# Hybrid decoder block with expert retrieval: 64 tokens instead of 32 get their down products by gathers, and 32 of the last block's dots are done in the top-16 stage

## The chip, the cores and the metric

The kernel runs on 1 core of a Trainium2 chip (trn2). The metric is device time in microseconds (us) of one execution; the profile shows one such execution.

The engines are PE (TensorE, matmuls; its weight loads are listed as PEld), DVE (VectorE), ACT (ScalarE), POOL (GpSimd) and SP (SyncE, which only issues transfers). Sixteen DMA engines move data for the queues of SP, ACT and POOL.

## The reference, cut to what matters

512 tokens of width 1024 go through an attention layer and then through a retrieval layer, which is the part that the change touches:

```
def peer_ffn(h, w_query, sub_keys_1, sub_keys_2, expert_down, expert_up):
    q = (ht @ w_query).reshape(N, PEER_HEADS, 2, PEER_QDIM // 2)      # N 512, 8 heads
    s1 = einsum('nhd,kd->nhk', q[:, :, 0], sub_keys_1)                # 128 keys
    s2 = einsum('nhd,kd->nhk', q[:, :, 1], sub_keys_2)
    t1, i1 = top_k(s1, 16);  t2, i2 = top_k(s2, 16)
    cand = t1[..., :, None] + t2[..., None, :];  sc, pos = top_k(cand, 16)
    eidx = (i1 * 128 + i2) at pos                                     # 128 * 128 = 16384 experts
    gate = softmax(sc)
    ...
        u = expert_down[e_c]                                          # rows of 1024
        a = gelu(einsum('cd,chkd->chk', x_c, u))
        vv = expert_up[e_c]
        return einsum('chk,chkd->cd', g_c * a, vv)
```

Each token picks 16 experts in each of 8 heads, 128 in all. For each it needs a dot product of its own vector with the expert's down row, a gelu, a gate, and the sum of the weighted up rows.

## The kernel before

Tokens lie in four blocks of 128. The last block (tokens 384 to 511) is handled by **gathers**: POOL fetches the picked down row of each of the 128 tokens (one indirect transfer of 128 rows, 512 KB), DVE takes the dot with the token's own vector (`dot`, or `pick` with kind "D"), and later POOL fetches the up rows and DVE adds them up (`pick` with kind "U"). The first three blocks (TD = 384 tokens) are handled **densely**: PE multiplies all 16384 experts with these tokens, 128 experts at a time (`score_block`), and the gate stage builds from one-hot matrices which of the products count.

The last XT = 32 tokens of the third block are a mixed case: their down products are not taken from the dense products but by gathers and dots as well, so `score_block` has TN = 384 - 32 = 352 token columns. XG = 128 / XT of their picks share a transfer, one per group of XT partitions, so these tokens cost XP = 128 / XG = 32 gathers ("X" picks). What they need is their gelu'd dots, moved back to their own partitions (`x_act`), multiplied into the gates (`x_w`) and put in place by one-hot matmuls of three bf16 parts instead of two f16 parts (`one_hots_extra`).

The stages around the change, in order of time:

- **The top-16 stage** (300 to 500 us). PE runs 16 rounds of query products, key scores and one `score_block` (numbers 2 to 17), then further blocks alone. DVE finds the top 16 of each head, eight heads one after the other, and the row numbers. `slots_T` on PE, in the middle of block E_SLOTS, transposes the result of the last head; only then can DVE make one-hot matrices.
- **The gate stage** (518 to 778 us): 12 groups of 32 tokens. Per group DVE makes four one-hot or weighted matrices of 128 x 4096 f16 (`one_hots`), PE multiplies them (64 matmuls) and runs some score blocks, `early_to(i)` says how far; ACT copies the gates out and stores them. Between the matrices DVE does the blocks' low parts (`d_low`) and the early dots.
- **The up stage** (778 to 1487 us): PE adds the up products of two numbers e per pair (`add_up`, 18 matmuls of 512 columns each), DVE makes their weights (`w_e`, `w_lo_e`) and low parts (`u_lo`), and the rest of the last block's picks; `units_by(e)` sets how many picks are done by number e. From number NE on, the pair also holds two score blocks and their `d_low`.

Every block e is three products: high part of the weights with high and low part of the tokens (L2050, 16 matmuls), low part of the weights with the high part of the tokens (L2062, 8). The high part is a rounding copy on ACT (`d_high`), and the low part is what is left. There are three ways to make it: DVE subtracts (`d_low`, blocks from E_DVE on), POOL subtracts (`early_low`), or, for ACC_FROM <= f < ACC_TO, ACT writes the negated rounded weights into `d_sum` and a POOL-issued transfer adds `d_raw` to it on its way (an **accumulate**, L660):

```
                if summed(f):
                    pool.wait_ge(S("d_hi_done"), f + 1)
                    pool.dma_start(d_sum[f % 3][:], d_raw[f % DR][:], accum_op=ALU.add)\
                        .then_inc(S(f"f_summed{f % 3}"), 16)
                    return
```

All queues are written out by hand and run in that order; nothing is scheduled. `d_raw` has 4 buffers (DR), `d_hi` and `d_sum` 3, gathered rows 4 in the gate stage (`e_in`) and 8 in the up stage (`p_in`). Block f's weights are loaded once block f - 4 is done; its high part is made once block f - 3 is done.

## Time and profile before

| | before |
|---|---|
| median of 3 runs | 1490.92 us (1490.85 to 1492.23) |
| the profiled execution | 1488.97 us, span 1487.2 us, granted clock 0.998 |
| PE / DVE / ACT / POOL busy | 98% / 82% / 42% / 37% of the span |
| moved by DMA | 412.08 MB, mean 277 GB/s |
| score blocks before the gates / up to the up stage / in it | 29 / 53 / 46 |
| gathers in the gate stage / in the up stage | 48 / 240 |

The span is from the first to the last instruction; the execution's own time is 1.8 us longer. A busy PE is not a PE at its peak, since its matmuls are pipelined: the distance between the starts of two matmuls is what one costs, not its duration. DMA share is the mean over the 16 engines of the time in which packets were under way; it can exceed 1 a little, since packets overlap.

### The profile page before, as it was taken

What the parts mean: (1) busy time and instruction counts of PE and PEld (TensorE: products, weight loads), DVE (VectorE), ACT (ScalarE), POOL (GpSimd) and SP (SyncE); (2) the same over time, 40 slices, a digit from 0 to 9 for tenths busy, and PEclk for the clock granted to TensorE, in tenths of its full rate; (3) what the DMA queues carried; (4) which work ended last, traced back from release to release, by engine and by line L of the source; (5) the groups of instructions that cost most, each with busy time, mean ns of one, the idle gap of its engine ahead of it and who ended that gap; (6) DMA issues with size and microseconds to landing.
All of it is one profiled execution on the core that took longest, in us unless ns stands there. A gap on an engine that the chain in (4) does not pass through costs nothing.

```text
span 1487.2 us, 22558 instructions
## 1 busy us (share of the span) xinstructions
PE 1459.3 (98%) x8412; PEld 1301.0 (87%) x8412; DVE 1220.5 (82%) x2396; ACT 629.3 (42%) x1003; POOL 551.8 (37%) x369
## 2 busy tenths in 40 slices
PE   9999999999999999999899999999999999999998
PEld 6887888798989999999897888888888998998996
DVE  5577886439999989998937888888879999999996
ACT  6237675343332445454543333333334334334334
POOL 0324101132312444543004444454426565667530
PEclk9999999999999999999999999999999999999999
DMA  7403003275555699999779999999999999999971
GB/s 308 163 1 114 1 1 131 70 191 167 166 142 145 220 346 389 377 373 356 295 274 394 387 378 370 382 360 384 377 412 331 400 373 409 368 403 380 392 283 71
DMA packets 140541, 412.08 MB, mean 277 GB/s; under 512 B 13553, under 2 KB 62321, under 8 KB 137489
## 3 DMA queue, kind: packets, MB, share of 16 engines
q1 hardware_dynamic: 81920, 206.08, 37.3%
q0 software_dynamic: 44256, 164.25, 30.3%
q10 hardware_dynamic: 14256, 40.31, 7.4%
q8 instruction: 67, 1.10, 0.3%
q14 instruction: 42, 0.34, 0.1%
HBM read 358.57 MB, written 42.04 MB: 269 GB/s over the span
## 4 chain that ended last, share of the span: by engine, by line
PE 81%; DVE 9%; DMA 6%; ACT 2%; issue 1%; SPq 0%; ACTq 0%; DVEq 0%
PE bank L2152 22%; PE bank L2050 16%; PE bank L1771 12%; PE bank L2158 11%; PE bank L2062 8%; DMA d_raw<-down 3%; PE bank L2122 3%; PE bank L1982 2%; PE bank L1966 1%; DMA w_raw<-wts 1%; PE bank L1891 1%; DVE gp L1645 1%; DMA a_e<-act_dram 1%; PE bank L2071 1%; DVE e_in L1586 1%
## 5 line engine op out<-in xcount | busy, mean ns | idle before, releaser
L2050 PE MATMUL bank<-h_hi,d_hi 128*128 128x352 f32 x1024 | 330.6, 324 | 2.8 <-ACT f_act L950 1.8
L2050 PE MATMUL bank<-h_lo,d_hi 128*128 128x352 f32 x1024 | 327.9, 321 | 0.0
L702 POOL DMA_INDIRECT p_in<-up,p_row x128 | 181.4, 1417 | 155.2 <-DVE xt L1677 76.5
L702 POOL DMA_INDIRECT p_in<-rows,p_row x112 | 163.9, 1463 | 180.4 <-DVE p_dot L1671 67.3
L2050 PEld LDWEIGHTS bank<-h_hi,d_hi 128*128 128x128 f32 x1024 | 191.7, 187 | 4.3 <-issue 3.3
L2050 PEld LDWEIGHTS bank<-h_lo,d_hi 128*128 128x128 f32 x1024 | 191.7, 187 | 1.1
L2152 PE MATMUL bank<-u_hi,w_hi_e 128*128 128x512 f32 x750 | 191.1, 390 | 1.0 <-DVE w_lo_e L1704 1.0
L2152 PE MATMUL bank<-u_hi,w_lo_e 128*128 128x512 f32 x750 | 190.6, 389 | 0.0
L2158 PE MATMUL bank<-u_lo,w_hi_e 128*128 128x512 f32 x750 | 190.5, 389 | 0.0
L1677 DVE SCALAR_TENSOR_TENSOR xt<-p_in,p_w,xt 128x1024 f32<-128x1024 f32 x128 | 164.2, 1283 | 6.8
L918 ACT ACTIVATE d_hi<-d_raw 128x1024 fp32r<-128x1024 f32 x128 | 132.4, 1053 | 87.6 <-DMA d_raw<-down 66.9
L2152 PEld LDWEIGHTS bank<-u_hi,w_lo_e 128*128 128x128 f32 x750 | 140.8, 188 | 29.8
L2158 PEld LDWEIGHTS bank<-u_lo,w_hi_e 128*128 128x128 f32 x750 | 140.8, 188 | 29.2
L2152 PEld LDWEIGHTS bank<-u_hi,w_hi_e 128*128 128x128 f32 x750 | 140.1, 188 | 29.1 <-ACT u_hi L998 1.3
L1570 DVE TENSOR_TENSOR u_lo<-u_raw,u_hi 128x1024 fp32r<-128x1024 f32 x128 | 152.4, 1221 | 13.4 <-ACT u_hi L998 13.4
L2062 PE MATMUL bank<-h_hi,d_lo 128*128 128x352 f32 x888 | 160.1, 321 | 0.0
L1575 DVE TENSOR_TENSOR d_lo<-d_raw,d_hi 128x1024 fp32r<-128x1024 f32 x102 | 122.5, 1221 | 35.1 <-ACT d_hi L918 35.1
L1040 ACT ACTIVATE w_hi_e<-w_e 128x768 fp32r<-128x768 f32 x64 | 54.3, 848 | 221.7 <-DVE w_e L1697 220.9
L2062 PEld LDWEIGHTS bank<-h_hi,d_lo 128*128 128x128 f32 x888 | 145.0, 187 | 0.0
L998 ACT ACTIVATE u_hi<-u_raw 128x1024 fp32r<-128x1024 f32 x128 | 130.2, 1048 | 19.2 <-PE bank L2158 18.1
L1671 DVE CUSTOM_DVE_ANT_0 p_in<-p_in,h_row 128x1024 f32<-128x1024 f32 x112 | 132.9, 1222 | 0.0
L1697 DVE TENSOR_TENSOR w_e<-a_e,g_e 128x768 f32<-128x768 f32 x64 | 61.3, 957 | 68.5 <-DMA a_e<-act_dram 38.7
(328 smaller groups left out, 2412.0 us busy)
## 6 DMA issues: line engine op xcount, KB each, us to landing
d_raw<-down SPq DMA_DIRECT2D x128, 512.0 KB, 6.9
u_raw<-up SPq DMA_DIRECT2D x128, 512.0 KB, 6.8
gates_dram<-ev ACTq DMA_DIRECT2D x12, 2048.0 KB, 7.0
g_e<-gates_dram SPq DMA_DIRECT2D x60, 384.0 KB, 9.1
w_raw<-wts SPq DMA_DIRECT2D x9, 2048.0 KB, 9.0
act_dram<-f_act ACTq DMA_DIRECT2D x82, 176.0 KB, 5.9
a_e<-act_dram SPq DMA_DIRECT2D x41, 352.0 KB, 8.1
d_sum<-d_raw POOLq DMA_DIRECT2D x17, 512.0 KB, 5.3
```

Source lines behind the costliest of these rows:

```text
L702: pool.indirect_dma_start(out=p_in[n % GR][:], out_offset=None, in_=rows if kind == "D" else up.rearrange("n p d -> (n p) d"), in_offset=b ...
L918: nc.scalar.activation(d_hi[e % DH_R][:], d_raw[e % DR][:], ACT.Copy).then_inc(S("d_hi_done"), 1)
L998: nc.scalar.activation(u_hi[e % UH][:], u_raw[e % UR][:], ACT.Copy).then_inc(S("u_hi_done"), 1)
L1570: V.tensor_tensor(u_lo[e % UR][:], u_raw[e % UR][:], f32(u_hi[e % UH][:]), ALU.subtract)\
L1575: V.tensor_tensor(d_lo[e % DR][:], d_raw[e % DR][:], f32(d_hi[e % DH_R][:]), ALU.subtract)\
L1671: V.tensor_tensor_reduce(out=rows_in[:], in0=rows_in[:], in1=h_row[:], scale=1.0, scalar=0.0, op0=ALU.mult, op1=ALU.add, accum_out=p_dot[: ...
L1677: V.scalar_tensor_tensor(xt[:, TDB], rows_in[:], p_w[:, p:p + 1], xt[:, TDB], ALU.mult, ALU.add)\
L1771: m = nc.tensor.matmul(out, a, b, start=(n == 0 and j == 0), stop=(n == last and j == 2))
L2050: nc.tensor.matmul(bank[6 + e % 2][:, 0:TN], d_hi[e % DH_R][:, k], h[:, k, 0:TN], start=(k == j == 0), stop=False)
L2062: m = nc.tensor.matmul(bank[6 + e % 2][:, 0:TN], low[:, k], h_hi[:, k, 0:TN], start=False, stop=(k == KC - 1))
L2152: nc.tensor.matmul(bank[2 * b + half][:], w[e // 2 % 2][:, e % 2, b * P:(b + 1) * P], u_hi[e % UH][:, half * COLS:(half + 1) * COLS], star ...
L2158: m = nc.tensor.matmul(bank[2 * b + half][:], w_hi_e[e // 2 % 2][:, e % 2, b * P:(b + 1) * P], u_lo[e % UR][:, half * COLS:(half + 1) * CO ...
```

## The change

XT becomes 64: TN falls to 320 columns, the X picks become XP = 64 gathers in two groups of partitions, and two of the twelve gate groups (instead of one) are made of three parts. The down dots of the last block's first two heads (EARLY_D = 32 instead of 16, out of the last block's 128) move out of the gate stage into the top-16 stage: DVE works out their rows after heads 0 and 1 (`t_row`), POOL gathers them into three new buffers (`t_in`) between its other work, and DVE takes the dots between the steps of heads 2 to 7. `slots_T` moves from block 24 to block 39, the accumulates cover blocks 3 to 35 instead of 3 to 19, and the first eight gate groups hold six blocks instead of five, so that NE goes from 82 to 104 and 24 instead of 46 blocks are left for the up stage. The up stage's picks fall from 240 to 224 and their plan changes.

```
-XT = 32
+XT = 64
 XG = P // XT
 XP = PICKS // XG
 TN = TD - XT
 XGRP = NTG - XT // TG
-EARLY_D = 16
-E_PICKS = [("D", p) for p in range(4)] + [("X", n) for n in range(XP)] + [("D", p) for p in range(4, EARLY_D)]
+EARLY_D = 32
+E_PICKS = [("D", p) for p in range(EARLY_D)] + [("X", n) for n in range(XP)]
+def e_slot(m):
+    return m % 3 if m < EARLY_D else (m - EARLY_D) % 4
+def gather_at(m):
+    return 8 + m * 3 // 5 if m < 21 else 20 + (m - 21) * 8 // 5
+def dots_at(n):
+    return range(EARLY_D * n // 18, EARLY_D * (n + 1) // 18) if n >= 0 else ()
...
-X_GELU = X_GROUPS
+X_GELU = X_GROUPS - 1
...
-E_SLOTS = 24
+E_SLOTS = 39
 E_DVE = E_SLOTS + 2
 E_GATES = E_SLOTS + 5
-ACC_FROM, ACC_TO = DH_R, 20
+ACC_FROM, ACC_TO = DH_R, E_SLOTS - 3
...
-    return E_GATES + 5 * min(i, X_GROUPS) + 2 * max(0, i - X_GROUPS)
+    return E_GATES + 6 * min(i, X_GROUPS) + 2 * max(0, i - X_GROUPS)
...
-        return max(0, e - 3) * 6 // 5
+        return max(0, e - 3) * 10 // 7
     last = NK - 4
-    start = (NE - 4) * 6 // 5
+    start = (NE - 4) * 10 // 7
     return min(len(ORDER), start + -(-(e - NE + 1) * (len(ORDER) - start) // (last - NE)))
...
             for f in range(E_DVE):
                 early_low(f)
+                for m in range(EARLY_D):
+                    if gather_at(m) == f:
+                        if m % TOPK == 0:
+                            pool.wait_ge(S("t_rows"), m // TOPK + 1)
+                        if m >= 3:
+                            pool.wait_ge(S("x_used"), m - 2)
+                        gather(m)
...
             pool.wait_ge(S("rows_ready"), 1)
-            for m, (kind, p) in enumerate(E_PICKS):
+            pool.wait_ge(S("x_used"), EARLY_D)
+            pool.wait_ge(S("pd_done"), ACC_TO)
+            pool.wait_ge(S("x_moved"), 16 * (2 * XG - 1))
+            for m in range(EARLY_D, len(E_PICKS)):
...
                 for f in range(early_to(i), early_to(i + 1)):
                     early_step(f)
+                    if f == early_to(X_GELU) + 4:
+                        extra_gelu()
...
+                    for m in dots_at(3 * hd - 6 + s):
+                        dot(m)
...
+                for m in dots_at(3 * hd - 4):
+                    dot(m)
...
+                if hd < EARLY_D // TOPK:
+                    dve.wait_ge(S("key_done"), 2 * hd + 2)
+                    V.scalar_tensor_tensor(t_row[:, hd * TOPK:(hd + 1) * TOPK], key[0][:, TDB, hd], float(NK), key[1][:, TDB, hd],
+                                           ALU.mult, ALU.add).then_inc(S("t_rows"), 1)
...
                 def between(n):
                     for _ in range(n):
+                        for _ in range(2 if i == X_GROUPS else 1):
+                            if dots:
+                                dot(dots.pop(0))
                         if lows:
                             d_low(lows.pop(0))
-                        if dots:
-                            dot(dots.pop(0))
```

Left out of this diff are the places of small tiles in SBUF and the semaphore counts that go with `e_slot`.

What POOL's queue holds around the end of the 16 rounds, before: `d_sum` are accumulates, `d_lo` are subtractions on POOL itself, and `e_in` the first early gathers, which stand behind all of them.

```order
L660 DMA d_sum_204<-d_raw_197 128x1024
L660 DMA d_sum_202<-d_raw_199 128x1024
L660 DMA d_sum_203<-d_raw_201 128x1024
L664 TENSOR_TENSOR d_lo_194<-d_raw_195,d_hi_207 128x1024
L664 TENSOR_TENSOR d_lo_196<-d_raw_197,d_hi_205 128x1024
L664 TENSOR_TENSOR d_lo_198<-d_raw_199,d_hi_206 128x1024
```

The same queue in the changed kernel, from block 24 on: `t_in` are the gathers of the last block's first two heads.

```order
L690 DMA d_sum_206<-d_raw_199 128x1024
L714 DMA t_in_148<-rows,t_row 128x1024
L690 DMA d_sum_207<-d_raw_201 128x1024
L690 DMA d_sum_208<-d_raw_203 128x1024
L714 DMA t_in_176<-rows,t_row 128x1024
L690 DMA d_sum_206<-d_raw_205 128x1024
L690 DMA d_sum_207<-d_raw_199 128x1024
L714 DMA t_in_177<-rows,t_row 128x1024
L690 DMA d_sum_208<-d_raw_201 128x1024
L714 DMA t_in_148<-rows,t_row 128x1024
```

From block 20 to block 35 every low part is now an accumulate with gathers between them, and POOL subtracts itself only from block 36 on.

DVE's queue for one gate group, before, from the second matrix on: `oh` and `gp` are the matrices, `e_dot` rows are the dots (each with a row that reads the accumulator).

```order
L1640 TENSOR_TENSOR oh_215<-iota_k,sl_key_175 128x4096
L1575 TENSOR_TENSOR d_lo_200<-d_raw_201,d_hi_207 128x1024
L1586 ISA e_in_233,e_dot<-e_in_233,x_home 128x1024
L1575 TENSOR_TENSOR d_lo_194<-d_raw_195,d_hi_205 128x1024
L1586 ISA e_in_230,e_dot<-e_in_230,x_home 128x1024
...
L1643 TENSOR_TENSOR gp_218<-oh_214,sl_g_176 128x4096
L1575 TENSOR_TENSOR d_lo_196<-d_raw_197,d_hi_206 128x1024
...
L1645 TENSOR_TENSOR gp_219<-oh_214,sl_g_177 128x4096
```

And in the changed kernel, from the third matrix of a group on:

```order
L1703 TENSOR_TENSOR gp_224<-oh_220,sl_g_180 128x4096
L1537 ISA e_in_237,e_dot<-e_in_237,x_home 128x1024
L1646 TENSOR_TENSOR d_lo_204<-d_raw_205,d_hi_211 128x1024
L1537 ISA e_in_234,e_dot<-e_in_234,x_home 128x1024
L1646 TENSOR_TENSOR d_lo_198<-d_raw_199,d_hi_209 128x1024
L1537 ISA e_in_235,e_dot<-e_in_235,x_home 128x1024
L1646 TENSOR_TENSOR d_lo_200<-d_raw_201,d_hi_210 128x1024
L1537 ISA e_in_236,e_dot<-e_in_236,x_home 128x1024
...
L1537 ISA e_in_237,e_dot<-e_in_237,x_home 128x1024
...
L1705 TENSOR_TENSOR gp_225<-oh_220,sl_g_181 128x4096
```

A group holds eight dots and six low parts instead of six and five, the dot now stands ahead of the low part, and the last five dots of a group stand close together, over a ring of four `e_in` buffers.

## Rows read from the trace of the kernel before

**Rows 1.** The page, busy time of PE, its weight loads and DVE.

```profile
PE 1459.3 (98%) x8412; PEld 1301.0 (87%) x8412; DVE 1220.5 (82%) x2396; ACT 629.3 (42%) x1003; POOL 551.8 (37%) x369
```

**Rows 2.** Busy time by stretch; the last columns are granted clock, DMA share, GB/s.

```profile
466.00:500.00 34.00, 31.62 (x202) 31.28 (x200) 33.62 (x151) 14.46 (x18) 14.78 (x6) 1.00 0.60 176
...
518.00:704.00 186.00, 184.35 (x1473) 182.36 (x1470) 168.78 (x168) 91.23 (x145) 85.10 (x44) 1.00 0.96 367
...
778.00:1102.00 324.00, 323.05 (x1427) 267.29 (x1427) 267.42 (x298) 110.33 (x122) 137.45 (x98) 1.00 1.01 382
1102.00:1436.00 334.00, 334.00 (x1767) 303.48 (x1766) 309.38 (x341) 120.02 (x154) 206.90 (x143) 1.00 0.99 381
```

**Rows 3.** Chain that ended last: start us, us, what; blocks and gate groups.

```profile
618.85 2.56 PE bank L2050 x16
621.41 1.28 PE bank L2062 x8
...
680.70 3.69 PE bank L2122 x64
...
744.63 7.21 PE bank L2122 x96
```

**Rows 4.** The same chain in the up stage.

```profile
861.63 2.72 PE bank L2152 x12
...
865.71 2.72 PE bank L2152 x12
```

**Rows 5.** Timeline of DVE at the end of the top-16 stage.

```profile
489.35 3.48 DVE L1454 TENSOR_TENSOR hit<-place_h,ranks 128x1024 f16<-128x1024 f16 x2
...
499.45 0.69 DVE L1553 TENSOR_TENSOR score<-score,g_sum 128x512 f32<-128x512 f32 x1
```

**Rows 6.** DMA queues from 357 to 364 us: packets, MB, share; issues, median landing.

```profile
q0 software_dynamic: 144, 0.52, 37.8%
q1 hardware_dynamic: 144, 0.52, 30.1%
q10 hardware_dynamic: 144, 0.18, 7.0%
...
d_sum<-d_raw POOLq DMA_DIRECT2D x1, 512.0 KB, 6.1
```

**Rows 7.** DMA queue of the gathers, 1102 to 1436 us; and the fastest 24.5 us.

```profile
q0 software_dynamic: 20437, 74.42, 58.1%
...
1236.00:1260.50 24.50, 24.50 (x133) 22.42 (x133) 23.13 (x21) 8.40 (x13) 15.06 (x14) 1.00 1.03 415
```

**Rows 8.** Timeline of DVE in a gate group; landing of the early gathers.

```profile
564.22 2.29 DVE L1638 TENSOR_TENSOR oh<-iota_k,sl_key 128x4096 f16<-128x4096 f16 x1
566.42 1.22 DVE L1575 TENSOR_TENSOR d_lo<-d_raw,d_hi 128x1024 fp32r<-128x1024 f32 x1
567.55 1.22 DVE L1586 CUSTOM_DVE_ANT_1 e_in<-e_in,x_home 128x1024 f32<-128x1024 f32 x1
568.70 2.29 DVE L1640 TENSOR_TENSOR oh<-iota_k,sl_key 128x4096 f16<-128x4096 f16 x1
...
e_in<-rows,e_row POOLq DMA_INDIRECT x32, 9.9
```

**Rows 9.** Timeline in the up stage, one pair: DVE, and PE's next block.

```profile
1162.35 0.96 DVE L1697 TENSOR_TENSOR w_e<-a_e,g_e 128x768 f32<-128x768 f32 x1 [0.98 <-ACT a_e L1035]
1163.23 1.28 DVE L1677 SCALAR_TENSOR_TENSOR xt<-p_in,p_w,xt 128x1024 f32<-128x1024 f32 x1
1164.42 0.99 DVE L1704 TENSOR_TENSOR w_lo_e<-w_e,w_hi_e 128x768 fp32r<-128x768 f32 x1
1165.34 2.35 DVE L1575 TENSOR_TENSOR d_lo<-d_raw,d_hi 128x1024 fp32r<-128x1024 f32 x2
...
1169.87 0.32 PE L2050 MATMUL bank<-h_hi,d_hi 128*128 128x352 f32 x1
1169.88 8.22 DVE L1677 SCALAR_TENSOR_TENSOR xt<-p_in,p_w,xt 128x1024 f32<-128x1024 f32 x6
```

More of the change, by code:

```diff
@@ L676, in w_low, with gather @@
                 ins.then_inc(S("w_part_lo"), 1)
+            def gather(m):
+                kind, p = E_PICKS[m]
+                slot = e_slot(m)
+                early = m < EARLY_D
+                rows_at = t_row if early else e_row
+                pool.indirect_dma_start(
+                    out=(t_in if early else e_in)[slot][:], out_offset=None, in_=rows,
+                    in_offset=bass.IndirectOffsetOnAxis(ap=rows_at[:, p:p + 1], axis=0)).then_inc(S(f"p_loaded{slot}"), 16)
             for f in range(E_DVE):
                 early_low(f)
+                for m in range(EARLY_D):
[5 more added lines that the diff above has]
+                        gather(m)
                 n, part = divmod(f - E_AHEAD, 4)
@@ L998, in u_high, with extra_gelu @@
                 nc.scalar.activation(u_hi[e % UH][:], u_raw[e % UR][:], ACT.Copy).then_inc(S("u_hi_done"), 1)
+            def extra_gelu():
+                last = slice(P - XT, P)
+                act.wait_ge(S("x_used"), len(E_PICKS))
+                nc.scalar.activation(e_act[0:P - XT], e_dot[0:P - XT], ACT.Gelu).then_inc(S("x_gelu"), 1)
+                nc.scalar.activation(x_act[last, PICKS - XP:], e_dot[last], ACT.Gelu).then_inc(S("x_gelu"), 1)
+                act.wait_ge(S("x_gelu"), 1)
+                for g in range(XG - 1):
+                    act.dma_start(x_act[last, g * XP:(g + 1) * XP], e_act[g * XT:(g + 1) * XT])\
+                       .then_inc(S("x_moved"), 16)
             for i in range(NTG):
@@ L1476, in keys_of, with dot @@
                      .then_inc(S("key_done"), 1)
+            def dot(m):
+                kind, p = E_PICKS[m]
+                slot = e_slot(m)
+                by_k = lambda t: t[:].rearrange("p (k d) -> p k d", k=KC)
+                to, own = (e_dot, x_home) if kind == "X" else (p_dot, by_k(h_row))
+                rows_in = by_k((t_in if m < EARLY_D else e_in)[slot])
+                dve.wait_ge(S(f"p_loaded{slot}"), e_loads(m, slot))
+                if (kind, p) == ("X", 0):
+                    dve.wait_ge(S("x_homed"), 16)
+                V.tensor_tensor_reduce(out=rows_in, in0=rows_in, in1=own, scale=1.0, scalar=0.0,
+                                       op0=ALU.mult, op1=ALU.add, accum_out=to[:, p:p + 1])\
+                 .then_inc(S("x_used"), 1)
             def top16(vals, idx, src, tmp):
```

62 lines of the change are left out of this document (24 added, 38 removed).

## The prediction

> **What bounds the kernel now.** I read the page first: PE is busy for 98% of the span [rows 1]. The reader is to see in that row that the weight loads leave room and that DVE, at 82%, is the next engine. The busy time by stretch then shows where each engine stands [rows 2]: PE works without a gap from 1102 to 1436 us, loses 1 us from 778 to 1102 and 2.4 us from 466 to 500, where it waits for the top-16 stage. In the same rows the DMA share is 0.96 in the gate stage and about 1 in the up stage, at 367 to 382 GB/s, and DVE is busy for 309 of 334 us in the second half of the up stage. So PE sets the end, and two resources stand right behind it. The chain that ended last gives PE's true prices, since it lists what one piece adds: a score block is 2.56 + 1.28 = 3.84 us for 24 matmuls of 352 columns, 160.2 ns each [rows 3]. In the up stage 12 matmuls of 512 columns add 2.72 us, 226.7 ns each, and one expert number takes 4.08 us (865.71 - 861.63) [rows 4]. The difference is 66.5 ns for 160 columns, 0.416 ns a column.
>
> **What PE gains.** 32 columns fewer take 13.3 ns from each matmul of a block: 24 x 128 = 3072 matmuls, **-41.0 us**. A block then costs 3.52 us. A gate group of three parts takes PE 7.21 us where one of two parts takes 3.69 [rows 3]; there is one more: **+3.5 us**. The 2.4 us wait at the old place of `slots_T` [rows 2] should go, because 15 more blocks of 3.52 us (53 us) stand before it, while DVE gets 32 dots of 1.15 us (37 us): **-2.4 us**. That DVE no longer meets POOL's subtractions (the pair of f16 products took 3.48 us at 489 us, beside them) [rows 5] only makes DVE earlier, and I give it nothing. DVE ended this work at about 500 us [rows 5]; with 37 us more it ends at about 537. PE had come to the middle of block 24 about 2.4 us before DVE's end, near 497.5; 24.5 blocks that are 0.32 us shorter and 15 more of 3.52 bring it to the middle of block 39 at 497.5 - 7.8 + 52.8 = 542, if nothing stops it.
>
> **What stops it: the accumulates, +25 us.** Blocks 20 to 35 now run back to back and each needs an accumulate, where before all but two of those after the rounds were subtracted on POOL. The DMA queues of one round show their price [rows 6]: in 7 us the accumulate's queue (q0) held the engines for 37.8%, 2.65 us, for 0.52 MB; the weight load (q1) for 2.1 us; the store of the products (q10) for 0.49 us. Nothing else ran, and the accumulate landed 6.1 us after its issue. A saturated queue of gathers costs 58.1% of 334 us for 143 gathers, 1.36 us each, and the fastest long stretch moved 415 GB/s at a share of 1.03 [rows 7]. A block of this stretch thus asks for 2.65 us (accumulate), 0.524 MB / 415 GB/s = 1.26 us (its load, taken at the saturated rate since the queues are full then), 0.44 us (store of 320 columns) and 11 gathers / 16 blocks x 1.36 = 0.94 us: 5.29 us, or 5.1 us at a share of 1.03, against PE's 3.52. Sixteen blocks lose 16 x 1.6 = 25 us. The rings of 3 and 4 buffers let it run two or three blocks ahead, so little can be saved up. PE stands in L2062 meanwhile, and behind it wait `slots_T`, then DVE with the whole gate stage; DVE's own last dots wait too, for gathers that stand behind the accumulates in POOL's queue. Bounds: 0, if accumulates overlap with other packets, and 16 x (6.2 - 3.52) = 43 us with the load at its 2.1 us and the store at 0.49.
>
> A rule speaks for a much lower price. The Trainium skill (DMA: Bandwidth & Descriptors, Bandwidth) says that transfers from SBUF to SBUF are bound by the fabric at 435 GB/s; by that an accumulate holds the engines for an estimated 1.2 us, not 2.65, and this term would be 4 us. The row contradicts it here: 0.52 MB in 2.65 us is about 200 GB/s.
>
> **The gate stage, +16 us.** A matrix costs DVE 2.20 us from start to start (564.22 to 566.42), a low part 1.13 and a dot 1.15 [rows 8]. Before: 4 x 2.20 + 5 x 1.13 + 6 x 1.15 = 21.4 us a group, against PE's 3.69 + 5 x 3.84 = 22.9. After: 8.8 + 6 x 1.13 + 8 x 1.15 = 24.8 us against 3.69 + 6 x 3.52 = 24.8. DVE's slack is gone. Yet it cannot run without stops: it idled 17.2 us in the eight groups of before [rows 2], 2.1 us each, for high parts whose weights come through a ring of four. These stops had lain in the slack; now each pushes the next matrices. I take 2 us x 8. Bounds: 0, if a later DVE finds its high parts ready, and 27 us from the ring of four gather buffers: the last dot of a group follows the one four before it by 3 x 2.28 + 1.15 = 8.0 us in DVE's order, but a freed buffer is full only 9.9 us after the next issue [rows 8], 11.4 us with the dot and the hand-over: 3.4 us x 8. The new waits behind the dots (`extra_gelu` on ACT) stand where all dots are done; nothing for them.
>
> **The up stage, +2 and +12 us.** First part: 10/7 instead of 6/5 picks a number, 2.86 a pair. DVE needs 0.88 + 0.92 + 2 x 1.13 + 2.86 x 1.17 = 7.4 us of 8.16 [rows 8, 9]; the transfers (two up loads, gates, products, gathers) are 3.27 MB in 8.16 us, 400 GB/s, between the 382 of this stretch now and the best 415 [rows 2, 7]: +2, bounds 0 and 11 (at 390 GB/s). Second part: 82 picks in ten pairs, 32 dots and 50 up rows. Up rows in a row cost 8.22 / 6 = 1.37 us each [rows 9]. DVE: 32 x 1.15 + 50 x 1.37 + 10 x (1.80 + 4 x 1.13) = 168.5 us; PE: 10 x (8.16 + 7.04) = 152. DVE may fall about 5 us behind before PE notices, since it starts a pair's low parts at 1165.34 and PE's next block starts at 1169.87 and needs the low part 2.6 us later, less the product's time [rows 9]: +12, bounds 5 and 17.
>
> **Sum**, against the profiled execution (1488.97 us; its span is 1487.2): -41.0 + 3.5 - 2.4 + 25 + 16 + 2 + 12 = +15, 1504 us. The median shown lies 1.95 us above that execution: **1506 us**, slower by 1.0%.
>
> **The rivals.** (a) An accumulate costs the engines no more than a copy, 1.26 us: a block asks 3.8 us, the term is 4 and the time 1485. For it: the measured round was partly idle. Against it: its queue alone held them 2.65 us. This is the case by the Trainium skill's fabric rule named above. It decides from a block of 3.95 us: below that the change is faster by over 0.2%. (b) The top-16 stage slips, but gate and up stage keep PE's pace but for 5 us: -41.0 + 3.5 - 2.4 + 25 + 5, 1481 us. For it: DVE stops for high parts because it comes early. (c) Nothing slips but a few us at the end: the columns' gain stays, 1454 us. For it: shares near 1 have not stopped PE so far. (d) The upper bounds come together in the top-16 and gate stages: 43 + 27 instead of 25 + 16, 1535 us.
>
> **How the numbers follow.** Forecast 0.46 (its own range 1492 to 1522), (a) 0.13, (b) 0.12, (c) 0.15, (d) 0.14. A measurement of this kernel tells about 0.2% from no change. Faster: all of (b) and (c), most of (a): 0.34; same: 0.08, from the edges of (a) and the forecast; slower 0.58. The range reaches from the upper part of (c) to the lower part of (d): 1458 to 1528.
>
> **What would show it.** Right: blocks 20 to 35 start about 5 us apart with PE waiting for the transfer into `d_sum`; DMA share about 1 there; the transposes of `slots_T` near 567 us; gate groups 26 to 28 us apart; PE gaps for `d_lo` or `w_lo_e` in the last ten pairs before the end. Wrong: blocks 3.5 us apart in that stretch and transposes near 542 us would take away the largest loss; gate groups at 24.8 us apart the second. If `score_block`'s matmuls do not come 147 ns apart, the gain itself was mis-sized.

## The result

The changed kernel takes **1546.93 us** (median of 4 runs, 1542.98 to 1548.80) against 1490.88 us: ratio **1.0372**, 95% interval 1.0357 to 1.0387. It is slower by 3.7%, where 1.0% was forecast, and it lies beyond the range (1458 to 1528 us). The profiled execution took 1547.79 us, with a span of 1545.9 us.

The page of the changed kernel (busy time, then the DMA total), beside [rows 1]:

```profile
PE 1441.7 (93%) x8444; PEld 1275.7 (83%) x8444; DVE 1245.9 (81%) x2448; ACT 642.0 (42%) x1019; POOL 616.5 (40%) x416
DMA packets 153454, 441.80 MB, mean 286 GB/s; under 512 B 14688, under 2 KB 69088, under 8 KB 150400
```

PE's busy share falls from 98 to 93%: the columns were saved and more than given back in waits. The view of one source line shows where. Each row has the first and the last start of a matmul: the transposes of `slots_T`, the gate matmuls, and the up stage's first product.

```profile
L2164 PE MATMUL bank<-cst,score x3: 421/421/476, 589.0 to 589.4; 128*128 128x128 f32 x3
L2182 PE MATMUL bank<-gp,oh x640: 218/218/308, 606.7 to 852.8; 128*128 128x128 f16 x160
L2212 PE MATMUL bank<-u_hi,w_hi_e x750: 387/389/472, 904.9 to 1523.6; 128*128 128x512 f32 x188
```

The same rows of the kernel before:

```profile
L2104 PE MATMUL bank<-cst,score x3: 272/273/329, 500.2 to 500.5; 128*128 128x128 f32 x3
L2122 PE MATMUL bank<-gp,oh x704: 217/218/233, 517.9 to 734.0; 128*128 128x128 f16 x176
L2152 PE MATMUL bank<-u_hi,w_hi_e x750: 387/389/467, 778.6 to 1464.8; 128*128 128x512 f32 x188
```

That cuts the span into three stages. "Without losses" is the length before, with the blocks between the two marks counted anew (3.84 us each out, 3.52 in: 53 and 60 in the gate stage, 46 and 24 in the up stage) and 3.5 us for the third part; for `slots_T` it is the prediction's 542.

| stage | before | without losses | after | lost | forecast |
|---|---|---|---|---|---|
| `slots_T` at | 500.2 | 542 | 589.0 | 47 | 25 |
| first gate matmul to up stage | 260.7 | 271.9 | 298.2 | 26 | 16 |
| up stage, first to last | 686.2 | 594.0 | 618.7 | 25 | 14 |

All three lost more than forecast, and the first misses most, 22 us. So most runs went there.

What engines waited for from 465 to 605 us in the changed kernel (total us, times, longest):

```profile
POOL d_sum L690 <- ACT d_hi L963: 63.9, 16, 12.7
DVE t_in L1537 <- DMA t_in<-rows,t_row: 42.2, 8, 9.6
PE bank L2122 <- DMA d_sum<-d_raw: 24.7, 10, 5.5
PE bank L2164 <- DVE score L1624: 5.5, 1, 5.5
```

In the changed kernel's numbering L2122 is a block's product with its low part (L2062 before), L2110 the one with its high part (L2050 before), and L2164 the transposes. Both PE and DVE stand still there: PE for accumulates, DVE for its gathers. ACT's timeline gives the blocks one by one, since each has one high part. Blocks 19, 20, 22, 23, 35 and 39:

```profile
456.25 1.04 ACT L963 ACTIVATE d_hi<-d_raw 128x1024 fp32r<-128x1024 f32 x1
...
472.67 1.04 ACT L963 ACTIVATE d_hi<-d_raw 128x1024 fp32r<-128x1024 f32 x1
...
482.62 1.04 ACT L963 ACTIVATE d_hi<-d_raw 128x1024 fp32r<-128x1024 f32 x1
496.27 1.05 ACT L963 ACTIVATE d_hi<-d_raw 128x1024 fp32r<-128x1024 f32 x1
...
557.45 1.04 ACT L963 ACTIVATE d_hi<-d_raw 128x1024 fp32r<-128x1024 f32 x1
...
574.99 1.06 ACT L963 ACTIVATE d_hi<-d_raw 128x1024 fp32r<-128x1024 f32 x1 [0.46 <-DMA d_raw<-down]
```

From 23 to 35 a block takes 61.18 / 12 = **5.10 us**, the forecast's number. But block 20 is late, there is a hole of 13.65 us before block 23, and `slots_T` comes 14 us behind block 39's high part.

Why block 20 is late can be read from PE's timeline, here the key scores of two rounds (eight matmuls, the same work both times):

```profile
463.60 2.08 PE L2131 MATMUL bank<-sk,q_sb 128*128 128x128 f32 x8 [3.67 <-DVE ti L1556]
...
470.60 1.05 PE L2131 MATMUL bank<-sk,q_sb 128*128 128x128 f32 x8
```

PE waits 3.7 us for DVE, which is late in the rounds, and then works slowly for a while: the key scores take 1.0 us more than the next ones, and the 16 matmuls on the high part behind them 1.6 us more than those of the next block (3.92 and 2.35 us). The granted clock from 464 to 468 us was 0.50, and 1.00 from 472 to 476 us. Wait and slow clock together are 6.3 us, and block 20 comes 6.4 us later behind block 19 than the rounds' usual 10.0 us.

### The profile page after: what moved, and what is told of

Read it like the earlier page. It is cut to its first block, busy times and chain, and to the rows that moved or that the text cites. A ratio compares the mean times of both kernels' runs of the same rounds, so it can differ in the third digit from the quotient of the medians.

```text
span 1545.9 us, 22788 instructions
## 1 busy us (share of the span) xinstructions
PE 1441.7 (93%) x8444; PEld 1275.7 (83%) x8444; DVE 1245.9 (81%) x2448; ACT 642.0 (42%) x1019; POOL 616.5 (40%) x416
## 4 chain that ended last, share of the span: by engine, by line
PE 46%; DVE 26%; DMA 19%; issue 3%; POOL 2%; ACT 2%; SPq 1%; DVEq 0%; ACTq 0%
PE bank L2212 14%; PE bank L1831 8%; PE bank L2218 7%; DMA a_e<-act_dram 5%; PE bank L2110 5%; DMA e_in<-rows,e_row 5%; DVE xt L1737 4%; DMA d_raw<-down 3%; PE bank L2122 3%; DVE d_lo L1646 3%; DVE e_in L1537 3%; PE bank L2042 2%; POOL p_in L747 2%; DMA t_in<-rows,t_row 2%; DMA d_sum<-d_raw 2%
## 5 line engine op out<-in xcount | busy, mean ns | idle before, releaser
L2110 PE MATMUL bank<-h_hi,d_hi 128*128 128x320 f32 x1024 | 310.8, 316 | 17.3 <-ACT d_hi L963 14.9
L2110 PE MATMUL bank<-h_lo,d_hi 128*128 128x320 f32 x1024 | 306.2, 312 | 0.0
L747 POOL DMA_INDIRECT p_in<-up,p_row x128 | 189.9, 1484 | 149.5 <-DVE xt L1737 68.6
L2110 PEld LDWEIGHTS bank<-h_hi,d_hi 128*128 128x128 f32 x1024 | 196.2, 192 | 22.7 <-ACT d_hi L963 20.5
L747 POOL DMA_INDIRECT p_in<-rows,p_row x96 | 157.6, 1642 | 117.0 <-DVE p_dot L1731 49.6
L2110 PEld LDWEIGHTS bank<-h_lo,d_hi 128*128 128x128 f32 x1024 | 196.4, 192 | 0.1
L2212 PEld LDWEIGHTS bank<-u_hi,w_hi_e 128*128 128x128 f32 x750 | 139.5, 188 | 38.5 <-ACT u_hi L1043 10.4
L2218 PEld LDWEIGHTS bank<-u_lo,w_hi_e 128*128 128x128 f32 x750 | 140.8, 188 | 29.2
L714 POOL DMA_INDIRECT e_in<-rows,e_row x64 | 103.4, 1616 | 131.8 <-DVE e_dot L1537 122.2
L2122 PE MATMUL bank<-h_hi,d_lo 128*128 128x320 f32 x760 | 128.8, 312 | 6.1 <-DVE d_lo L1646 6.1
L1646 DVE TENSOR_TENSOR d_lo<-d_raw,d_hi 128x1024 fp32r<-128x1024 f32 x87 | 104.7, 1220 | 24.9 <-ACT d_hi L963 24.8
L2122 PEld LDWEIGHTS bank<-h_hi,d_lo 128*128 128x128 f32 x760 | 116.7, 190 | 6.9 <-DVE d_lo L1646 6.9
L1731 DVE CUSTOM_DVE_ANT_0 p_in<-p_in,h_row 128x1024 f32<-128x1024 f32 x96 | 114.4, 1217 | 4.5 <-DMA p_in<-rows,p_row 4.5
```

What stands on the lines that cost most here:

```text
L747: pool.indirect_dma_start(out=p_in[n % GR][:], out_offset=None, in_=rows if kind == "D" else up.rearrange("n p d -> (n p) d"), in_offset=b ...
L1646: V.tensor_tensor(d_lo[e % DR][:], d_raw[e % DR][:], f32(d_hi[e % DH_R][:]), ALU.subtract)\
L1731: V.tensor_tensor_reduce(out=rows_in[:], in0=rows_in[:], in1=h_row[:], scale=1.0, scalar=0.0, op0=ALU.mult, op1=ALU.add, accum_out=p_dot[: ...
L2110: nc.tensor.matmul(bank[6 + e % 2][:, 0:TN], d_hi[e % DH_R][:, k], h[:, k, 0:TN], start=(k == j == 0), stop=False)
L2122: m = nc.tensor.matmul(bank[6 + e % 2][:, 0:TN], low[:, k], h_hi[:, k, 0:TN], start=False, stop=(k == KC - 1))
L2212: nc.tensor.matmul(bank[2 * b + half][:], w[e // 2 % 2][:, e % 2, b * P:(b + 1) * P], u_hi[e % UH][:, half * COLS:(half + 1) * COLS], star ...
```

## The experiments

All times are medians; "ratio" is that to the kernel before, which was run again beside them (medians 1488.79 to 1491.18 us). The stage lengths come from the same three rows as above. Runs are of the changed kernel with the edit named. The stage lengths are those of one profiled execution, whose time lies up to 6.7 us from the median of its run (e1_pool_sub 1531.99 us, e2_even 1535.70, e20_paced_25 1492.39), so a difference of a few us between two stage lengths says little by itself. Three runs leave work out to price it: e4_copy the addition, e7_no_gathers 29 of the 32 early gathers, e18_nog_copy both.

| run | us | ratio, interval | `slots_T` at | gate stage | up stage |
|---|---|---|---|---|---|
| changed kernel | 1546.93 | 1.0372 (1.0357 to 1.0387) | 589.0 | 298.2 | 618.7 |
| e1_pool_sub | 1538.64 | 1.0333 (1.0315 to 1.035) | 575.9 | 298.9 | 614.6 |
| e4_copy | 1528.90 | 1.0283 (1.0254 to 1.0313) | 568.9 | 295.0 | 619.0 |
| e2_even | 1530.78 | 1.0273 (1.0256 to 1.029) | 587.1 | 283.9 | 621.5 |
| e3_iota | 1548.07 | 1.0385 (1.0364 to 1.0407) | 589.0 | 297.6 | 620.1 |
| e7_no_gathers | 1517.96 | 1.0203 (1.0167 to 1.0239) | 559.8 | 296.6 | 617.4 |
| e5_alt_even | 1525.47 | 1.0247 (1.0215 to 1.0278) | 574.0 | 286.6 | 619.3 |
| e6_slope32 | 1540.00 | 1.0319 (1.0278 to 1.036) | 590.5 | 296.3 | 610.7 |
| e9_slope43 | 1553.28 | 1.0417 (1.0391 to 1.0443) | 586.3 | 296.5 | 628.3 |
| e10_deep_ring | 1541.72 | 1.0343 (1.0319 to 1.0368) | 582.0 | 301.2 | 619.4 |
| e11_deep_even_slope | 1515.00 | 1.0178 (1.0159 to 1.0196) | 580.0 | 283.5 | 610.7 |
| e12_deep_even_slope_alt | 1507.84 | 1.0126 (1.0103 to 1.0149) | 575.6 | 283.9 | 609.7 |
| e13_xt32 | 1534.96 | 1.0295 (1.027 to 1.0319) | 589.9 | 278.0 | 626.1 |
| e18_nog_copy | 1507.00 | 1.0108 (1.0079 to 1.0136) | 551.5 | 298.5 | 619.6 |
| e15_half_early | 1511.02 | 1.015 (1.0113 to 1.0188) | 549.3 | 289.7 | 633.0 |
| e16_half_early_28 | 1502.76 | 1.0091 (1.0065 to 1.0116) | 528.3 | 292.5 | 638.5 |
| e17_half_early_alt | 1506.13 | 1.0118 (1.0081 to 1.0155) | 540.9 | 289.8 | 636.1 |
| e19_paced | 1498.39 | 1.0046 (1.0029 to 1.0062) | 524.9 | 288.4 | 647.8 |
| e20_paced_25 | 1498.02 | 1.0063 (1.0037 to 1.0089) | 513.2 | 285.1 | 651.8 |

### What an accumulate costs

**e1_pool_sub**: POOL subtracts blocks 20 to 35 again.

```
-ACC_FROM, ACC_TO = DH_R, E_SLOTS - 3
+ACC_FROM, ACC_TO = DH_R, 20
```

> The changed kernel with the accumulates given back for blocks 20 to 35: POOL subtracts there, as it did before the change; all else as changed. Theory A (an accumulate holds the DMA engines for 2.65 us or more, so blocks 23 to 35 stand 5.1 us apart): without them a block asks the engines for 2.6 us, the blocks go at PE's 3.5 to 3.7 us, 12 x 1.5 = 18 us are saved there, and the transposes of slots_T come near 568 us instead of 589: 1547 - 20 = 1527 us (1520 to 1535; DVE loses some us beside POOL's subtractions). Theory B (the accumulates are not what holds the stretch, but the loads behind the late constants or DVE's wait for its own gathers): under 6 us saved, 1541 or more.

`slots_T` came 13 us earlier, at 576 instead of the expected 568, and the median fell by 8 us, less than theory A's 12 to 27 and more than theory B's 6: neither theory. The windows of this run (PE, PEld, DVE, ACT, POOL busy; clock; DMA share; GB/s) show that another engine took over:

```profile
520.00:540.00 20.00, 17.64 (x121) 17.38 (x119) 19.96 (x58) 7.50 (x10) 9.83 (x5) 0.99 0.78 255
540.00:560.00 20.00, 14.44 (x85) 14.44 (x86) 19.93 (x79) 4.93 (x7) 18.10 (x9) 0.75 0.56 171
```

DVE is busy without a gap and the DMA engines are at 0.56 to 0.78. DVE waited 1.7 us for its gathers from 465 us on, instead of 42.2, and PE waited 7.0 us for DVE's `score` at `slots_T`; 14.4 us more it waited for POOL's low parts, which stand in POOL's queue behind gathers that wait for DVE's dots (up to 10.4 us). The same work takes DVE longer beside POOL's subtractions; the line that adds up the candidates, for one, here and in the changed kernel:

```profile
L1576 DVE TENSOR_TENSOR cand<-tv,tv 128x64 f32<-128x64 f32 (+1 forms) x40 | 20.6, 579 | 0.1
```
```profile
L1576 DVE TENSOR_TENSOR cand<-tv,tv 128x64 f32<-128x64 f32 (+1 forms) x40 | 8.5, 277 | 0.1
```

In all, DVE was busy 301 us from 200 us to `slots_T`, against 275. So the way out of the accumulates costs DVE 26 us in a stage where it has none to spare.

**e4_copy**: the same transfer without adding.

```
-pool.dma_start(d_sum[f % 3][:], d_raw[f % DR][:], accum_op=ALU.add)\
+pool.dma_start(d_sum[f % 3][:], d_raw[f % DR][:].bitcast(F32R))\
```

> The changed kernel, but each accumulate is a plain copy of the same 0.52 MB between the same two tiles (the low part of a down matrix is then wrong: nothing is added). Theory A as I wrote it in the prediction, with the accumulate as something dearer than a copy (2.65 against 1.26 us of the engines): blocks 23 to 35 come 3.9 us apart instead of 5.1, 12 x 1.2 = 14 us less, 1533 us (1528 to 1538). Theory C (it is the transfer from SBUF to SBUF through this queue that costs about 2.65 us, whether it adds or not): blocks still 5 us apart, 1543 to 1549 us.

20 us earlier at `slots_T`, and 1529 us lies in theory A's range: it is the adding that costs, not the way from SBUF to SBUF. Theory C is out. The gathers stand in the same queue, so the price was taken in a pair of runs without them:

**e7_no_gathers** and **e18_nog_copy** (the latter with the copy besides):

```
-                    if gather_at(m) == f:
+                    if gather_at(m) == f and m < 3:
```

> The changed kernel without 29 of the 32 early gathers: the 32 dots of the top-16 stage are all done, but from the fourth on over what stands in the three buffers, so the last block's first heads get wrong values. It tells which of two chains sets the transposes of slots_T. Theory A (the accumulates starve PE, and DVE's 50.7 us of waits for its gathers only fill time that PE loses anyway): slots_T moves only by what the gathers' bytes take from the DMA engines, about 11 x 1.36 = 15 us in that stretch, most of it hidden: slots_T at 578 to 584 us, 1535 to 1541 us. Theory D (DVE's chain sets it: it waits for gathers that stand in POOL's queue behind accumulates, which wait for high parts, which wait for loads): DVE now ends at about 540 us, PE alone decides, and slots_T comes at 563 to 575 us, when PE has block 39: 1520 to 1533 us.

> The changed kernel without 29 of the 32 early gathers (as in the run without gathers) and with plain copies for accumulates: the low parts and the first heads of the last block are wrong. Against the run without gathers (blocks 23 to 35 4.44 us apart, slots_T at 559.8 us, 1518 us) it gives the accumulate's price by itself. If a copy holds the engines 1.3 to 1.5 us, a block asks for 1.4 + 1.5 + 0.45 = 3.4 us: blocks at PE's 3.5 to 3.7 us, slots_T at 545 to 550 us, 1503 to 1508 us. If a copy costs as much as an accumulate, nothing changes: 1516 to 1520 us.

The queues from 480 to 530 us without gathers (packets, MB, share of 16 engines), q0 being accumulates alone and q1 the blocks' loads:

```profile
q0 software_dynamic: 1601, 5.84, 59.9%
q1 hardware_dynamic: 1671, 6.06, 34.0%
q10 hardware_dynamic: 1675, 1.90, 10.7%
```

and with copies:

```profile
q0 software_dynamic: 1781, 6.44, 36.2%
```

5.84 MB are 11.1 accumulates of 0.524 MB, in 0.599 x 50 = 30 us: **2.69 us each**. A copy: 18.1 us for 12.3, **1.47 us**. A load is 17.0 us for 11.6, also 1.47 us, and not the 1.26 that I took. An accumulate thus moves 195 GB/s and a copy 356. The Trainium skill (DMA: Bandwidth & Descriptors, Bandwidth) gives 435 GB/s for transfers within SBUF; the copy comes to four fifths of that, and the accumulate to under half, so for the accumulate the measured price decides. Rival (a) of the prediction falls with that.

### What the gathers cost

Without gathers `slots_T` comes at 559.8 us, 29.2 us earlier and earlier than either theory had it. Blocks 20, 22, 23, 35 and 39 of e7_no_gathers:

```profile
468.06 1.04 ACT L963 ACTIVATE d_hi<-d_raw 128x1024 fp32r<-128x1024 f32 x1
...
477.28 1.05 ACT L963 ACTIVATE d_hi<-d_raw 128x1024 fp32r<-128x1024 f32 x1
...
483.89 1.05 ACT L963 ACTIVATE d_hi<-d_raw 128x1024 fp32r<-128x1024 f32 x1
...
537.21 1.04 ACT L963 ACTIVATE d_hi<-d_raw 128x1024 fp32r<-128x1024 f32 x1
...
551.36 1.06 ACT L963 ACTIVATE d_hi<-d_raw 128x1024 fp32r<-128x1024 f32 x1 [0.46 <-ACT f_act L995]
```

So the 29 us are: 4.6 up to block 20 (in the changed kernel it stands 16.4 instead of 10.0 us behind block 19; of these 6.4 us 1.8 do not show, since this run's blocks are 1.8 us late from the start, before any gather); 0.7 from 20 to 22; 7.0 between 22 and 23 (6.6 instead of 13.65); 7.9 from 23 to 35 (4.44 us a block instead of 5.10); 3.4 from 35 to 39; and 5.6 behind block 39, where in the changed kernel PE waits 5.5 us for DVE's `score`. Only the third item stood in my sum, there with 0.94 us a block for the 0.66 measured. Two ways by which gathers cost were then separated, bytes and order.

**e10_deep_ring**: from the 22nd gather on a ring of eight buffers, in memory that the last projection has left.

```
-    return m % 3 if m < EARLY_D else (m - EARLY_D) % 4
+    return m % 3 if m < FAR else (m - FAR) % 8 if m < EARLY_D else (m - EARLY_D) % 4
...
-    return 8 + m * 3 // 5 if m < 21 else 20 + (m - 21) * 8 // 5
+    return 8 + m * 3 // 5 if m < FAR else 20 + m - FAR
```

> The changed kernel with eight instead of three buffers for the early gathers from the 22nd on (they lie where the last projection's weights lay, free once the 16 rounds are done), and these eleven gathers issued at blocks 20 to 30 instead of 20 to 36. Bytes, accumulates and dots are the same; only the order and the waits of POOL's queue change. Theory D (the gathers cost so much because POOL's queue ties DVE to PE: accumulates wait behind gathers that wait for dots, and dots wait for gathers that stand behind accumulates): slots_T at 568 to 575 us instead of 589, 1527 to 1534 us. Theory B2 (it is their bytes alone, 0.52 MB each on full DMA engines): slots_T at 583 or later, 1541 or more.

Between the two: 7 us. DVE now was done 26 us ahead and waited for ACT's exponentials, which stand in ACT's queue behind block 38:

```profile
DVE g_sum L1630 <- ACT score L1032: 25.9, 1, 25.9
PE bank L2130 <- DMA d_sum<-d_raw: 23.2, 12, 5.6
```

PE's own wait for accumulates stayed at 23 us. So DVE's chain (the order of POOL's queue) made up about 7 of the 29 us at the end of the stage. The other 22 us are then bytes and what the last rounds lose; no run parts these two.

**e3_iota** was a miss in my reading:

> The changed kernel with the load of iota_k (1 MB) issued at block 39 instead of block 22, that is after the stretch of accumulates instead of at its head. Theory A (the late constants stand ahead of the down loads in SP's queue, which put 13.7 us between the high parts of blocks 22 and 23 where later ones are 5.1 apart; the iota is two thirds of their bytes): block 23 comes 5 to 6 us earlier, the transposes of slots_T near 584 us, 1541 to 1543 us. Rival (the transposes wait for DVE, whose last dots wait for gathers, so that an earlier block 23 changes nothing): 1546 to 1548 us. A rise above 1549 would say that the iota now comes too late for the first gate matrix.

Nothing moved, and the hole before block 23 stayed (483.36 to 496.35 us). The rows of the two transfers in the changed kernel's DMA view from 474 to 497 us (KB, us from issue to landing) show why it could tell nothing:

```profile
x_home<-x_h SPq DMA_DIRECT2D x1, 512.0 KB, 18.0
iota_k<-consts_h SPq DMA_DIRECT2D x1, 64.0 KB, 17.0
```

The iota is 64 KB and not 1 MB; `x_home` is the large one. By itself it makes no hole either: in e18_nog_copy the same load stands there, and blocks 22 and 23 are 5.1 us apart (475.12 to 480.20).

The queues of the same stretch, 474 to 497 us, say more (packets, MB, share):

```profile
q0 software_dynamic: 864, 3.15, 57.9%
q1 hardware_dynamic: 1752, 2.67, 32.9%
q10 hardware_dynamic: 536, 0.60, 7.2%
```

The engines have hardly a gap: the shares add up to 98%. In that time three accumulates, three gathers, four blocks' loads and the two transfers above were issued, since the blocks follow each other faster once the rounds are over. Block 23's own load was issued at 478.73 us, right behind those two, and took 16.55 us. Over all runs the distance of blocks 22 and 23 goes with what is issued there: 9.9 to 14.7 us where accumulates and gathers are, 9.0 us with gathers alone (e1_pool_sub), 6.9 with gathers and copies (e4_copy), and 6.6 to 7.0 with accumulates alone.

**e15_half_early**, **e16_half_early_28**, **e17_half_early_alt**: 16 early dots whose gathers fall into the rounds, 32 or 28 blocks before `slots_T`, with the even spread and the 3/2 below; the third with POOL subtracting even blocks.

```
-EARLY_D = 32
+EARLY_D = 16
...
-E_SLOTS = 39
+E_SLOTS = 32
```

> A form of the change with 16 instead of 32 early dots (their gathers all fall into the 16 rounds, where the DMA engines have room), 32 instead of 39 blocks before slots_T, 16 more picks in the up stage, the even spread and 3/2 picks per expert. If the gathers hurt only behind the rounds: block 20 comes near 468 us as in the run without gathers, DVE ends 19 us earlier than with 32 dots, slots_T at 520 to 530 us for 7 blocks fewer; the work that is left for later is PE's own, so the sum is ideal 1451 plus about 10 in the top-16 stage, 10 in the gate stage, 20 in the up stage: 1490 to 1500 us. If 16 gathers among the rounds hurt as they did here and the up stage cannot carry 16 more picks: 1505 to 1515 us.

> As the run before, with 28 blocks before slots_T: four accumulated blocks fewer in the full stretch. If DVE's end (near 520 us) decides slots_T, PE with 28 blocks stands ready at about 510 us and waits some 10 us: 5 us slower than with 32 blocks. If the accumulates still decide, 3 to 5 us faster.

> As the run with 32 blocks, with the even ones of blocks 20 to 28 subtracted by POOL. A block asks for 3.4 us of the DMA engines instead of 4.7, so PE keeps its pace if DVE does: 3 to 8 us faster than with all accumulated. If DVE beside POOL's subtractions sets slots_T: the same, or up to 4 us slower.

1511, 1503 and 1506 us: each block fewer in the full stretch helps (28 against 32: 8 us, more than expected, and DVE again waited 22 us for the exponentials). But block 20's high part came at 485 to 488 us, not 468 (the expectation of e19_paced says 475, which is block 19). POOL's timeline of e16_half_early_28 says why:

```profile
431.12 1.03 POOL L714 DMA_INDIRECT t_in<-rows,t_row  x1 [1.08 <-DVE p_dot L1537]
447.20 0.98 POOL L714 DMA_INDIRECT t_in<-rows,t_row  x1 [15.05 <-DVE p_dot L1537]
448.15 1.04 POOL L690 DMA_DIRECT2D d_sum<-d_raw  x1
```

The gather at 447 us waited 15 us for the dot that frees its buffer, and behind it stood the accumulate that the next round's block needs.

**e19_paced** moves only this: gather m behind block 8 + m. **e20_paced_25** has 25 blocks before `slots_T` as well.

```
-    return 8 + m * 3 // 5 if m < 21 else 20 + (m - 21) * 8 // 5
+    return 8 + m
```

> As the run with 16 early dots and 28 blocks, but gather m stands behind block 8 + m in POOL's queue instead of 8 + 3m/5, so that the dot that frees its buffer is done when POOL comes to it. If the place in the queue was what cost: the rounds are 10 us apart to the end, the high part of block 20 comes at 466 to 468 us instead of 475, slots_T at 520 instead of 528, 1493 to 1497 us. If the bytes cost: no change, 1501 to 1504 us.

> As e19_paced with 25 blocks before slots_T. DVE stood done about 20 us before slots_T with 28; three accumulated blocks fewer there cost the full stretch 3 x 1.6 us less and come back later at PE's own 3.5 us: 1487 to 1493 us, about the kernel before. If DVE now decides slots_T: not faster than e19_paced.

The rounds are even again in e19_paced and block 20 comes in time:

```profile
459.31 1.04 ACT L963 ACTIVATE d_hi<-d_raw 128x1024 fp32r<-128x1024 f32 x1
...
469.29 1.04 ACT L963 ACTIVATE d_hi<-d_raw 128x1024 fp32r<-128x1024 f32 x1
```

Block 20 came 17 us earlier, but the hole before block 23 opened here too (479.60 to 493.21 us, where e16_half_early_28 had 7.0 us), and `slots_T` moved 3.4 us, the time 4.4. Gathers now stand behind blocks 20 to 23 in POOL's queue, where e16_half_early_28 had its last behind block 17. With 25 blocks DVE sets `slots_T` (PE waits 15.5 us for it), and the time stays at 1498; its twelve runs spread from 1489.85 to 1509.35 us, so it can't be told from e19_paced. These are the best forms found: 0.5 to 0.6% slower than the kernel before.

### The gate stage

**e2_even**: the same dots and low parts, two and two behind each matrix.

```
 V.tensor_tensor(oh[r][0][:], iota, cols(sl_key[0]), ALU.is_equal).then_inc(S("oh_a"), 1)
-between(1)
+between(2)
...
-between(max(len(lows), len(dots)))
+between(2)
 V.tensor_tensor(gp[r][1][:], oh[r][0][:], cols(sl_g[1]), ALU.mult).then_inc(S("oh_done"), 1)
+between(max(len(lows), len(dots)))
```

> The changed kernel with the same matrices, low parts and dots in the gate stage, but spread evenly: two dots and two low parts behind each of the four matrices of a group, where the changed kernel has one, two and then five dots in a row. Theory A (the gate groups stand 28.3 us apart instead of 24.8 because the fifth dot in a row needs a buffer of the ring of four that its gather has not filled): two dots per 6.7 us leave 12 us for a reload against 11.4 needed, the groups come 25 to 26 us apart, 8 x 2.5 to 3.3 = 20 to 26 us less: 1521 to 1527 us. Rival (the groups are slow because DVE's work of 24.8 us plus its waits for d_hi, or the DMA share of 0.9, fill them): 28 us apart as before, 1543 or more; slower by a few us if PE now gets its first matrix of a group later.

The chain of waits of the changed kernel, one group:

```profile
646.49 2.20 DVE gp L1703
648.68 1.14 DVE e_in L1537
...
650.10 10.13 DMA e_in<-rows,e_row
...
660.25 1.23 DVE e_in L1537
...
661.48 2.21 DVE gp L1705
```

The last dot of the group is done 12 us behind the one four before it, since its gather takes 10 us after that buffer is free. This holds in every group, 28.4 us apart (633.04, 661.48, 689.67). With the even spread PE's gate matmuls come:

```profile
606.28 3.69 PE bank L2183 x64
...
632.17 3.90 PE bank L2183 x64
...
658.71 3.69 PE bank L2183 x64
...
684.79 3.68 PE bank L2183 x64
...
692.08 9.43 DMA d_raw<-down
```

26.2 us apart, and the stage is 14.3 us shorter; the time, 1530.8 us, is 4 us above the expected range. The ring of four gather buffers was the cause of that part. What follows in the chain is the load of a block's weights, 9 to 10 us in a ring of four, so that this is the next limit; no run changed that ring. Both periods, 28.4 and 26.2 us, lie above DVE's and PE's 24.8 us.

**e5_alt_even** adds POOL's subtraction for even blocks from 20 on.

```
-    return ACC_FROM <= f < ACC_TO
+    return ACC_FROM <= f < ACC_TO and (f < 20 or f % 2 == 1)
```

> The changed kernel with two edits: of blocks 20 to 35 only the odd ones are accumulated, the even ones subtracted by POOL; and the even spread of the dots in the gate stage. Theory A: a block of this stretch asks the DMA engines for 5.3 - 2.65 / 2 = 4.0 us instead of 5.3; eight POOL subtractions cost DVE half of the 26 us that sixteen cost it (301 us busy up to slots_T against 275). slots_T at 565 to 572 us, 17 to 24 less than 589, and with the 16 us of the even spread 1507 to 1514 us. Rival (DVE beside POOL's subtractions becomes the bound as it did with all sixteen): slots_T at 576, 1518 to 1522 us.

5 us less than the even spread alone, and `slots_T` at 574, about where e1_pool_sub had it: half of the subtractions give as much there as all. `slots_T` lies between the theory's 565 to 572 us and the rival's 576, the time 3 us above the rival's range.

### The up stage

**e6_slope32** and **e9_slope43**: 3/2 or 4/3 instead of 10/7 in `units_by`.

> The changed kernel with 3/2 instead of 10/7 picks per expert in the first part of the up stage: 150 instead of 142 picks there, 74 instead of 82 in the last ten pairs. By the prediction's terms the last ten pairs lose 8 x 1.37 = 11 us of DVE's work there, of which up to 11 come off the time. If the first part (1.03 share of the DMA engines at 390 to 400 GB/s) has no room, it pays 8 x 0.52 MB / 400 GB/s = 10.5 us for them: net 1545 to 1549 us. If it has room, 1536 to 1540 us.

> The changed kernel with 4/3 instead of 10/7 picks per expert in the first part of the up stage: 133 instead of 142 there, 91 instead of 82 in the last ten pairs. If the first part's 9 us of PE's waits come from full DMA engines, 9 gathers fewer give nearly all of them back, while the last ten pairs get 9 x 1.37 = 12 us more: 1547 to 1552 us. If the first part's waits have another cause (the activations' loads come late in SP's queue whatever the bytes), only the 12 us are seen: 1556 to 1560 us.

The up stage is 8.0 us shorter with 8 picks fewer in the last ten pairs, and 9.6 longer with 9 more: 1.0 us for each pick that is moved. e6_slope32 comes out at 1540 us, the edge of what was expected if the first part has room (its four runs spread from 1531.5 to 1542.3 us); e9_slope43 lies at 1553, between its two ranges, and its first part gave back 1.9 us. The windows of the first part and of the last pairs, in the changed kernel and with 3/2:

```profile
905.00:1378.00 473.00, 463.75 (x2088) 384.80 (x2087) 412.55 (x465) 156.67 (x180) 262.55 (x166) 1.00 1.02 392
1378.00:1546.00 168.00, 147.99 (x795) 130.37 (x793) 151.95 (x173) 61.02 (x91) 87.16 (x61) 0.99 0.80 315
```
```profile
900.00:1375.00 475.00, 464.08 (x2085) 386.44 (x2084) 420.03 (x472) 156.15 (x179) 267.67 (x170) 0.99 1.02 396
1375.00:1538.00 163.00, 155.39 (x837) 138.31 (x835) 148.70 (x170) 63.18 (x93) 83.60 (x57) 0.99 0.81 322
```

PE's idle time in the first part hardly changes (9.3 and 10.9 us) although eight transfers more go through; in the last pairs it falls from 20.0 to 7.6 us. (Cut at the same distance from the up stage's first matmul, 905.7 to 1378.8 us, the second run has 10.9 us as well.) The first part had room that the profile's share of 1.02 did not show.

### The parts together

**e11_deep_even_slope**, **e12_deep_even_slope_alt**: the repairs, and with POOL's subtractions.

> The three repairs together: eight buffers for the late early gathers, the even spread of the gate stage's dots (16 us alone), and 3/2 instead of 10/7 picks per expert (7 us alone). If they add up with 15 us of the deeper ring: 1506 to 1512 us. If the even spread and the slope only move waits into DMA engines that are full, 1515 to 1525.

> The three repairs and, besides, the even ones of blocks 20 to 35 subtracted by POOL instead of accumulated. If the DMA engines still hold the top-16 stage in the run with three repairs, slots_T comes another 5 to 12 us earlier: 1496 to 1505 us. If DVE holds it there, it is the same or a few us later, since DVE works slower beside POOL's subtractions.

1515.0 and 1507.8, 3 us above the better range of the one and of the other. The three repairs take off 32 us together, and took off 5, 16 and 7 alone: they add up. With 32 early dots no form that does all the work brings `slots_T` below 574 us.

**e13_xt32**: the 32 tokens of before, all else as changed.

```
-XT = 64
+XT = 32
```

> The other part of the change alone: 32 tokens as before instead of 64 get their down products by gathers and dots (blocks of 352 columns, four dots in a gate group), with the 32 early dots, 39 blocks before slots_T and six in a gate group as changed. Against the changed kernel PE gets 3072 x 13.3 ns = 41 us more and 3.5 less, while the gate stage loses its 26 us (DVE has 20.2 us of work against PE's 26.7 in a group) and the up stage has 32 dots' bytes less to carry beside it. If the top-16 stage loses what it lost before, 40 us against PE's pace, 1540 to 1550 us: the 64 tokens bring as much as they cost. If the wider blocks of 3.84 us fill what the stage lost, 1515 to 1525 us: the 64 tokens alone cost 25 us.

1535.0, between the two ranges. The rest of the change (the moved dots and blocks, and the plan of the up stage) alone costs 45 us against the kernel before (`slots_T` at 590 here as well), and the 64 tokens another 12, although they take 37.5 us off PE's work.

## Why the prediction was off

**Columns, -41 us, and the third part, +3.5: right.** The chain has 16 matmuls in 2.35 us and 8 in 1.17 to 1.18, so a block takes 3.52 us; a group of three parts 7.26 us. (3.84 us for 24 matmuls are 160.0 ns each and not 160.2; the gain stays 13.3 ns.)

**Accumulates, +25 us: the mechanism and its price right, the stage wrong.** "2.65 us for 0.52 MB" was measured as 2.69, "5.1 us at a share of 1.03" as 5.10. The load was taken at 1.26 us and is 1.47, and the gathers at 0.94 us a block, where 0.66 was measured: that the sum hit 5.10 so closely is partly luck, since these two errors cancel. What failed is the step that the stage loses 16 times the difference and nothing else: 47 us were lost. The missing 22 are the 6.4 us before block 20 (3.7 of PE's wait for DVE, which is late in the rounds since it waits for gathers, and 2.6 of the lower clock behind that wait), 8.5 in the hole before block 23, 3.4 behind block 35, where no accumulate stands any more, and 5.5 at `slots_T`. These make 24; the 2 us more are within what one profiled execution tells.

**"-2.4 us" for the wait at the old place: wrong.** The text said that DVE "ends at about 537". Its work was sized well (42 us more from 200 us to `slots_T`, for 37), but it waited 50.7 us for its own gathers, with 10 us from issue to landing and a ring of three. 589 less these 50.7 is 538. I had named these gathers ("DVE's own last dots wait too") without giving them a price.

**Gate stage, +16 us: the taken value wrong, the bound right.** I took 2 us a group for late high parts. The groups came 28.4 us apart by the mechanism that I kept as the upper bound, "the ring of four gather buffers", 3.4 us a group, and 26 us were lost.

**Up stage, +2 and +12: the first mis-sized, the second right.** The first part lost 8 us more than before (9.3 of 473 us), near its bound of 11, and the last pairs 13 (20.0 idle against 6.8 in the same pairs before). The other 4 of the 25 us are not accounted for. Moving a pick was worth 1.0 us, below the 1.37 of an up row's own work.

**The range.** Of the three stages the first came above the upper bound that I gave it, and the two others just below theirs: 47 for 43, 26 for 27, 25 for 28. Rival (d) put two of these together and ended at 1535; the range cut it at 1528. With all three at their bounds the text's own numbers give 1549.

What stays open: how much of the hole of 13.6 us behind the rounds each transfer makes. The DMA engines are full in it, and it shrinks with the gathers and with the accumulates; the loads of `x_home` and `iota_k`, which my sum for this stretch left out, fall there too (`x_home` lands 18 us after its issue), and no run took them away. TensorE's clock had a mean of 0.986 here against 0.998 before; but for the 2.6 us before block 20, what it cost was not told apart from the waits around it.

## What to carry to other kernels

Work that is moved into a stage with idle engines takes its transfers with it: price them in that stage, in order, with the engine time of their kind and their time to land against the ring that holds them, not by bytes alone. Here the DMA engines were full and every queue ran in order, and one late item was paid by all the engines behind it; the losses of three stages came near their bounds together, so add such bounds up before you set a range. Spreading the dots evenly over a group costs nothing and was worth 16 us.
